# Recurrent pairs of a two-block model: every product in 64x64 quarters, right sides, solves and outputs in two row steps, and the odd group's first left blocks made on GpSimd

## What is computed

```python
def wkv7_scan(r, w, k, v, kk, a, reverse):
    def step(state, inp):
        r_t, w_t, k_t, v_t, kk_t, a_t = inp
        sa = jnp.einsum('bhij,bhj->bhi', state, -kk_t)
        state = (state * w_t[:, :, None, :] + sa[..., None] * (kk_t * a_t)[:, :, None, :]
                 + v_t[..., None] * k_t[:, :, None, :])
        return state, jnp.einsum('bhij,bhj->bhi', state, r_t)
...
y = direction(0, False) + direction(1, True)
...
branch = jnp.einsum('bsnc,ncd->bsnd', ys, w_branch)
gates = jax.nn.sigmoid(gl.reshape(b, s, N_BRANCH, D_MODEL) + b_gate)
merged = jnp.sum(gates * branch, axis=2)
```

## Time and profile before

| | us |
|---|---|
| median of 3 runs | 2549.43 (2548.84 to 2550.6) |
| the profiled execution, whole | 2548.45 |
| its span | 2546.7 |
| TensorE matmuls busy | 2484.2 (98% of the span) |
| VectorE busy | 1439.2 (57%) |
| ScalarE busy | 527.6 (21%) |
| GpSimd busy | 316.1 (12%) |
| the pairs of layer 0, from the first score to the first mean | 158.7 (195.0 to 353.7) |
| the pairs of layer 1 | 159.0 (829 to 988) |

### The profile page before, as it was taken

How to read it: one execution, slowest core, us unless ns; L and a number is a source line. 1 busy time by engine, 2 the same in 40 slices (tenths; PEclk the granted TensorE clock), 3 DMA queues, 4 the chain that set the end, 5 groups by cost and what they waited for, 6 DMA issues and landing times. The chain is left out here.

```text
span 2546.7 us, 38463 instructions
## 1 busy us (share of the span) xinstructions
PE 2484.2 (98%) x15968; PEld 1905.6 (75%) x15968; DVE 1439.2 (57%) x2688; ACT 527.6 (21%) x1249; POOL 316.1 (12%) x367
## 2 busy tenths in 40 slices
PE   8999999999999999999999999999999999999998
PEld 7887886854788788685477747888886666666997
DVE  1576655855157655573357735555334488854775
ACT  1342220100134222010014910000003243411000
POOL 2002102110100210221000000000000155410110
PEclk9999999999999999999999999999999999999999
DMA  7331125987433212598632022222222534334553
GB/s 269 116 116 63 57 81 170 303 292 256 147 116 117 68 52 84 179 306 289 239 125 67 2 66 71 96 83 75 91 87 69 165 101 135 121 102 146 167 173 107
DMA packets 253603, 341.80 MB, mean 134 GB/s; under 512 B 7252, under 2 KB 179412, under 8 KB 253304
## 3 DMA queue, kind: packets, MB, share of 16 engines
q1 hardware_dynamic: 241632, 311.71, 37.4%
q10 hardware_dynamic: 8920, 17.67, 2.1%
q0 software_dynamic: 2880, 9.96, 1.0%
HBM read 338.13 MB, written 1.19 MB: 133 GB/s over the span
## 5 line engine op out<-in xcount | busy, mean ns | idle before, releaser
L1058 PE MATMUL PS<-MEM 128*128 128x256 f32 (+1 forms) x2632 | 447.9, 332 | 2.6 <-ACT MEM L1515 1.2
L1058 PEld LDWEIGHTS PS<-MEM 128*128 128x128 f32 x2632 | 406.3, 190 | 43.8 <-issue 1.9
L416 PE MATMUL PS<-MEM 128*128 128x256 f32 x1632 | 356.0, 379 | 0.0
L1474 ACT ACTIVATE MEM<-PS 128x256 f32<-128x256 f32 (+4 forms) x405 | 162.0, 429 | 907.8 <-PE PS L416 221.1
L416 PEld LDWEIGHTS PS<-MEM 128*128 128x128 f32 x1632 | 308.6, 190 | 42.5 <-issue 1.3
L462 PE MATMUL PS<-MEM 128*128 128x512 f32 x608 | 265.4, 597 | 9.1 <-DMA MEM<-w_down 4.3
L2094 DVE SCALAR_TENSOR_TENSOR MEM<-MEM 128x512 f32<-128x512 f32 x280 | 214.4, 798 | 53.7 <-DMA MEM<-ada_w 48.0
L462 PEld LDWEIGHTS PS<-MEM 128*128 128x128 f32 x608 | 115.3, 191 | 155.3 <-issue 141.2
L3038 POOL TENSOR_TENSOR MEM<-MEM 128x1 f32<-128x1 f32 (+1 forms) x34 | 21.6, 637 | 1269.4 <-DVE MEM L2040 812.1
L696 PE MATMUL PS<-MEM 128*128 128x256 f32 x768 | 178.3, 384 | 0.0
L1371 PE MATMUL PS<-MEM 128*128 128x512 f32 (+1 forms) x512 | 171.5, 488 | 0.0
(11 more groups left out here) (384 smaller groups left out, 3259.8 us busy)
## 6 DMA issues: line engine op xcount, KB each, us to landing
MEM<-w_in SPq DMA_DIRECT2D x54, 1024.0 KB, 5.4
MEM<-ada_w SPq DMA_DIRECT2D x48, 1024.0 KB, 7.5
MEM<-w_up SPq DMA_DIRECT2D x32, 1024.0 KB, 5.4
MEM<-w_down SPq DMA_DIRECT2D x32, 1024.0 KB, 5.1
MEM<-ssm_w_in SPq DMA_DIRECT2D x24, 1024.0 KB, 5.4
MEM<-ffn_gate SPq DMA_DIRECT2D x22, 1024.0 KB, 5.3
MEM<-ffn_up SPq DMA_DIRECT2D x22, 1024.0 KB, 5.4
MEM<-ffn_down SPq DMA_DIRECT2D x20, 1024.0 KB, 5.1
```

What stands on the lines that cost most here:

```text
L416: ins = pe.matmul(bank[:, 0:T], W[:, k, c * P:(c + 1) * P], XT[:, k, :], start=k == 0, stop=k == KT - 1)
L1058: ins = pe.matmul(out, left[:, k, :], right[:, k, :], start=k == 0, stop=k == 3)
L1474: act.activation(out, view(b), func, **kw).then_inc(S("bank_read_by_act"), 1)
```

## The change

1. Every product inside the pairs uses a 64x64 quarter of the array, apart from the turned keys. `scores` splits the 128 weight columns in two. A fill step is four quarter products: two tiles are summed at once (`pair_of_tiles`), in banks 6 and 7. In the first turn tile 0 uses rows 0 to 63 of the contraction and tile 1 rows 64 to 127, for all k; in the second turn they change over. Between the turns TensorE waits for its own products (`half_summed`). A pair of gate tiles is 16 steps, of branch tiles 8.
2. `right_side`, `solve` and `outputs` are split by rows of the contraction (`right_first` and `right_second`, `solve_first` and `solve_second`, `outputs_first`, `_second`, `_third`), for both groups of the pair at once, with a wait for TensorE's own products (`row_step`) in between, so that two row halves never add into one place together. Quarters of the triangular matrices that are zero are left out. The right side of a group takes one bank instead of two, and one ScalarE copy of 256 columns instead of two of 128.
3. A slot stops when a pair of tiles is complete; the rest of its steps is owed to the next slot. `FILL_SLOT` has new numbers.
4. `begin_left` of the odd group of pairs 1 to 3 moves from VectorE to GpSimd, behind its first mask of that pair (`left`, `left_begun`).
5. VectorE reads both states of a pair before both outputs.

```diff
+    for turn in range(2):
+        if turn:
+            pe.wait_ge(S("half_summed"), halves[0])
+        for k in range(nk):
+            for j, b in enumerate(banks):
+                r = HB * (j ^ turn)
+                for o in (0, HB):
+                    ins = pe.matmul(PS[o:o + HB, b, 0:T], W[r:r + HB, k, (c + j) * P + o:(c + j) * P + o + HB], src[r:r + HB, k, :],
+                                    start=turn == 0 and k == 0, stop=turn == 1 and k == nk - 1)
...
-    tiles_in[l, pair, name] = sum(next(gate_run) for _ in range(FILL_SLOT[name][pair]))
+    owed[0] += FILL_SLOT[name][pair]
+    tiles = 0
+    while owed[0] and not tiles:
+        tiles += next(gate_run)
+        owed[0] -= 1
+    tiles_in[l, pair, name] = tiles
...
-    ins = pe.matmul(banks[half][:, 256 * j:256 * j + 256], BK[pb:pb + 64, d, ct, c, part, :], rhs, start=True, stop=True)
+    for o in (0, HB):
+        ins = pe.matmul(banks[half][o:o + HB, 256 * j:256 * j + 256], BK[pb:pb + 64, d, ct, c, part, o:o + HB], rhs, start=True, stop=True)
...
+def solve_first(gs):
+    for i in range(4):
+        for g in gs:
+            for o in (0, HB):
+                ins = pe.matmul(PS[o:o + HB, opened["sa", g], i * HB:(i + 1) * HB], AB[g % 4][o:o + HB, i, o:o + HB], RH[g % 2][o:o + HB, i, :],
+                                start=i == 0, stop=i == 3 and o == HB * (g % 2))
...
     cross_right(gs)
+    solve_first(gs)
     slot(pair, "XO")
-    for g in gs:
-        solve(g)
+    solve_second(gs)
+    outputs_first(gs)
     slot(pair, "sa")
-    for g in gs:
-        outputs(g)
+    outputs_second(gs)
+    outputs_third(gs)
...
+def left(l, g):
+    emptied(pool, ("dx", l, g - 2, LEVELS - 1))
...
+    for j, o in enumerate((0, HB)):
+        pool.tensor_tensor(u[o:o + HB, :, :], AB[g % 4][o:o + HB, :, o:o + HB],
+                                 LVL[o:o + HB, 1 - g % 2, 0, :].unsqueeze(1).to_broadcast([HB, 4, HB]), ALU.mult).then_inc(S("left_masked"), 1)
+        pool.wait_ge(S("left_masked"), n + j + 1)
+    pool.tensor_tensor(u[:, :, :], IDC.unsqueeze(1).to_broadcast([P, 4, HB]), u[:, :, :], ALU.subtract).then_inc(S("left_begun"), 1)
```

More of the change, by code:

```diff
@@ L691, in gate_tiles @@
                         W = a_slab(w_in[l], O_G + D * n + 256 * s)
[L692 to L703, removed]
+                        work = pair_of_tiles([("gl", l, n, 2 * s + c) for c in range(2)], "act", W, 0, XT, KT)
+                        yield from shut(work, 2)
                 def branch_tiles(n, Y):
@@ L708, in branch_tiles, with shut @@
                         W = b_slab(w_branch[l, n], 0, 512 * s)
[L709 to L720, removed]
+                        yield from pair_of_tiles([("br", l, n, 4 * s + c) for c in range(2)], "dve", W, 0, Y, 4)
+                        work = pair_of_tiles([("br", l, n, 4 * s + c) for c in (2, 3)], "dve", W, 2, Y, 4)
+                        yield from shut(work, 2)
+                def shut(work, tiles):
+                    for step in work:
+                        tiles -= step
+                        if tiles == 0:
+                            close_slab()
+                        yield step
                 def gate_work():
@@ L872, in cross_right @@
                                 done(ins)
[L874 to L878, removed]
-                        emptied(pe, ("st", l, g - 4))
-                    banks = [take(("rh", l, g, half), "act") for half in range(2)]
-                    o = [banks[i % 2][:, (i // 2) * 64:(i // 2 + 1) * 64] for i in range(4)]
-                    for half in range(2):
-                        for i, ct, pb, h in inst[half::2]:
-                            ins = pe.matmul(o[i], AK[i2][:, i, 0:P], VTK[:, c, 64 * h:64 * h + 64], start=i < 2, stop=wave == 0 and i >= 2)
-                        if wave == 0:
-                            done(ins)
-                    if wave == 1:
-                        for i, ct, pb, h in inst:
-                            ins = pe.matmul(o[i], KR[pb:pb + 64, d, ct, c, 0, :], ST[pb:pb + 64, d, ct, :], start=False, stop=i >= 2)
-                            if i >= 2:
-                                done(ins)
@@ new lines, in solve_second @@
+                def solve_second(gs):
+                    for g in gs:
+                        emptied(pe, ("XO", l, g))
+                    other_rows()
+                    for i in range(4):
+                        for g in gs:
+                            f = HB * (g % 2)
+                            r, b = HB - f, opened["sa", g]
+                            ins = pe.matmul(PS[r:r + HB, b, i * HB:(i + 1) * HB], AB[g % 4][f:f + HB, i, r:r + HB], RH[g % 2][f:f + HB, i, :],
+                                            start=False, stop=i == 3)
+                            if i == 3:
+                                numbered(("sa", l, g), "act", b)
+                                done(ins)
@@ new lines, in outputs_first @@
+                def outputs_first(gs):
+                    open_banks("y", gs)
+                    for i in range(4):
+                        for g in gs:
+                            d, c, wave, inst = instances(g)
+                            _, ct, pb, h = inst[i]
+                            f = HB * d
+                            to = PS[pb:pb + HB, opened["y", g], (i // 2) * P:(i // 2 + 1) * P]
+                            pe.matmul(to, VTK[f:f + HB, c, 64 * h:64 * h + 64], AK[g % 2][f:f + HB, i, P:2 * P], start=i < 2, stop=False)
+                            if wave and pb == f:
+                                pe.matmul(to, ST[pb:pb + 64, d, ct, :], KR[pb:pb + 64, d, ct, c, 1, :], start=False, stop=False)
@@ L3077, in _ @@
                             ins.then_inc(S("level_masked"), 1)
+                            if m == 1 and g % 2 and pair:
+                                left(l, g)
                 pool.wait_ge(S("merged"), l + 1)
```

183 lines of the change are left out of this document (139 added, 44 removed), and 6 rows, old and new, of the table FILL_SLOT.

## The result

The changed kernel takes 2564.73 us (median of 4 runs, 2562.9 to 2567.22), the kernel before 2549.14 (4 runs beside it, 2548.16 to 2550.6): ratio 1.0061, 95% interval 1.0044 to 1.0079. It is slower by 15.6 us, where 22 us faster were forecast, and it lies outside the range of 2500 to 2550.

A forecast was written before the change was run, and what follows sets the result against it. TensorE, busy 98% of the span, was taken as the bound. Per layer, 145.0 from the walk + 0.9 look-ahead + 1.7 clock = 147.6 for 158.7, saving 22.2 in both layers: 2527 us, range 2500 to 2550.

The forecast's parts named there:

- A fill step of 0.436 with four quarters of 256 columns: TensorE's fill: four quarter products of 256 columns run at once, so a step still takes 0.436 us.
- two-at-a-time rival: Fill and scores: quarters with 256 columns run only two at a time, stage 37 us longer, 2624 us; chance 0.11.
- The changes of 0.17: TensorE between runs of differing matmul shape: each change costs about 0.17 us; 20 us of them a layer go.
- 126 us a layer of work: TensorE in a layer's pairs: streams of 123.2 plus turned-key shape changes 0.8 and waits for itself 1.8.
- The walk: Pairs written down engine by engine in program order with latencies: sum 143.2 us a layer, 145.0 with 1.8 added.
- The pairs of layer 0: Forecast time of pairs 0 to 3: 43.1, 30.6, 32.2 and 35.6 us, plus 1.7 for 4 leftover fill steps.
- First Z: TensorE ahead of pair 0's first Z: idle grows from 1.64 to 4.9 us, then a half-speed clock costs 1.7.
- Bank waits in pair 3: Fill tiles ending in twos: 1.9 us lost at level 2's subtraction, 1.9 and 1.6 at slots z5 and W.
- Look-ahead: Outputs: quarter streams overlap only if TensorE looks ahead; 0.45 us a wave-1 pair charged, 0.9 a layer.
- GpSimd's part: Left blocks moved to GpSimd: 2.1 to 2.9 us, hidden before the next Z; VectorE's saving hidden too, so 0.
- The rule of one PSUM bank: Solve's first step: row tiles cannot share a bank, 1.88 instead of 0.94 us, 7.5 more in all; not charged.
- The rival "slower": Quarters with 256 columns run two at a time: 2624 us; chance 0.11, with any smaller slowdown over 2554.

The follow-up runs named there:

- the probe: Kernel before with 512 independent products of 64x64x64 added in a row behind the pairs of each layer: 2604.42 us, 55.8 over before.
- the probes: Kernel before with 512 independent quarter products added in each layer, in two runs: 64 moving columns each, 2604.42 us; 128 moving columns each, 2603.27 us.

## Why the prediction was wrong, step by step

- **A fill step of 0.436 with four quarters of 256 columns: right.** Four steps are 1.73 (L711 x32 from 195.55 to 197.28), where the two-at-a-time rival needed 3.5. The changes of 0.17 are gone too: L819 x16 runs in 0.86 to 0.88. PE's busy time fell by 9 and 13 us with them.
- **The step that failed** is the term "126 us a layer of work": streams added up as if an instruction cost only its columns, with nothing for the number of instructions. The change puts 4208 matmul records in a stage for 2880, and I counted products only to find the busiest quarter. The page of before had what was needed to ask: 15968 matmuls and 128 blocks on the instruction queue (now 18624 and 149). By the probe 34 blocks need 119 to 136 us if they come evenly, which is under 147.6; but TensorE doesn't use them up evenly. Pair 1 begins with 128 matmuls in 3.3 us (243.42 to 246.73), and the next 128 from 249.05 on take 3.2, both under the probe's 3.5. The densest 256 matmuls of layer 0 take 6.3 us now (from 240.9 on) and took 8.8 before. In layer 1, 422 matmuls run from 857.6 to 868.8, 3.4 us for 128, and there the pause of 2.31 follows (871.09): what is stored ahead didn't bridge such a run. Against the forecast of 147.6 the stages are 16.0 and 17.2 longer. Idle marked issue is 7.2 and 16.3 of that, where the forecast had none; in layer 0 two falls of the clock that weren't charged add up to 3.4, and the rest of that layer, some 5 us, lies in other waits, not parted further.
- **Other waits: sized about right.** The walk had 17.6 of idle a layer; the long starts that no block ended are 21.0 and 16.6, half-clock starts among them, and by chance a few more stand among those behind blocks.
- **The pairs of layer 0** were forecast at 43.1 plus 1.7 of clock, 30.6, 32.2 and 37.3 with the leftover. They took 49.6, 34.7, 40.2 and 39.1. Pair 0: 4.8 over, of it 2.6 behind blocks and 1.7 a second low clock, from 232.3 on. Pair 1: 4.1 over, of it 3.2 behind blocks. Pair 2: 8.0 over, of it 4.2 behind blocks, 1.7 a third low clock (314.2), and 1.4 a bank wait at 313.31 that took 2.4 where I had 1.
- **First Z:** idle of 4 to 5 and a clock of 0.50 behind it, right (4.10, and 3.4 us at 0.50 from 205.0 on). But I had charged 1.7 a layer for one such fall; layer 0 had three, after waits of 4.10, of 0.92 and 1.05 (229.65 and 231.61), and of 2.41 us (313.31). The granted clock of the four pairs (0.93, 1.00, 0.96, 1.00) says where. The rule of the Trainium skill (TensorE: Matmul & The Clock Gate, Part 1), that idleness brings the clock down, agrees with this in direction.
- **Bank waits in pair 3:** two of three right, 1.50 at 338.96 and 1.88 at 346.08; the 1.9 charged at level 2 doesn't show, the waits there are 0.46 (326.58) and less. Missed: the flipped keys wait 0.92 for the masks in pair 0 (229.65).
- **Look-ahead:** right. The three output steps of pair 0 take about 3.0 in all (240.4 to 243.4), and in pair 1 instructions of L1010, L1011 and L1013 alternate in the timeline at every 0.05.
- **GpSimd's part:** right at nothing when alone. No wait of TensorE is marked with `left`.
- **The rule of one PSUM bank** (the Trainium skill, TensorEngine Tiling, Gotcha 1): the solve's first step (L964) of pair 1 starts its 32 records within 0.93 (270.81 to 271.74), by the rule 1.88, and the first two start 0.01 apart. The trace still disagrees for halves on different partitions.
- **The rival "slower"** named one mechanism, columns two at a time, and it was the wrong one; the outcome fell into its tail, 0.11 for any slowdown over 2554. A rival for the cost of issuing 46% more instructions was missing, though a pause marked issue of 0.35 stood in the trace of before.

Open: the 3.8 us between and behind the stages. The page has L416 waiting 1.2 for its weights (0.0 in the earlier trace rows), which is a part of it; no run parted it further.

## What to carry to other kernels

Splitting a product into quarters keeps the columns per quarter and multiplies the instructions. Before doing it, divide a stretch's matmul records by 128 and its time by that: at 7.0 us (this kernel before) hardly anything was lost, at 5.0 (after) the denser stretches stood still, and under 3.5 to 4.0 TensorE waited for its own instructions all along, however few columns each had. Wide moving operands help, since 128 columns took no more time than 64 in the probes, and so does one full-array instruction in place of four.

And when fill and changes of shape go away, the waits that they covered come back; give the walk a column for each engine's latency and for the clock that may fall behind a wait.

## What the runs showed of the hardware

- Instruction blocks of 16384 bytes hold 128 matmuls with their weight loads (8 more blocks for the 1024 records of a probe's row). In layer 0 of the probes a transfer is 0.92 to 1.35 us, TensorE goes on 2.2 to 2.4 us behind its start, and blocks begin 3.3 to 4.0 us apart (seven distances in each: mean 3.76 and 3.53).
- 64x64 products of 64, 256 and 512 moving columns all run four at once: 0.0147 a record for 64 (L973 x128), 0.054 for 256, 0.107 for 512.
- In the changed kernel the clock fell to 0.50 for 3.4 us behind a wait of 2.41 us, and behind two of 0.92 and 1.05 close together, not only behind one of 3.6 as in the earlier trace rows; a wait of 2.31 us passed without it (871.09).
